# One row tile for both norm parts, weight loads ahead of the bias rows, a later strip load, and two early input chunks

## The reference, cut to what matters

```python
# first block, twice
h = rms_norm(x, norm_mix[l]); z = h @ w_in[l]
qa, ka, va, qi, ki, wi, cq, ckv, kr, ga, gb = split_cols(z)
qa, ka = rms_norm(qa), rms_norm(ka)              # per head of 64
y_a = sparse_indexed_attention(qa, ka, va, qi, ki, wi, rel_bias, 128)
cq, ckv = rms_norm(cq), rms_norm(ckv)            # latents of 384 and 256
qb, kb = up-projections, rope on 32 of 96, rms_norm per head of 96
y_b = latent_attention(qb, kb, vb)
x = x + (sigmoid(ga + ..) * (y_a @ w_proj_a) + sigmoid(gb + ..) * (y_b @ w_proj_b)) @ w_out[l]
h = rms_norm(x, norm_ffn[l]); u = causal_dwconv(h @ w_up[l], ..)
x = x + (silu(u[.., D_FF:]) * u[.., :D_FF]) @ w_down[l]
# second block, once: dilated attention, and attention over keys that are
# compressed (hid = gelu(blocks @ w1 + b1); keys = hid @ w2), selected, and in a window
# then gated feed-forward and a last rms_norm
```

## Time and profile before

| | us |
|---|---|
| median of three runs | 2419.99 |
| profiled execution | 2424.52 |
| its span, first to last instruction | 2422.7 |
| PE busy in the span | 2356.8 (97%) |
| POOL busy | 1592.8 (66%) |
| DVE busy | 1242.0 (51%) |
| ACT busy | 615.5 (25%) |
| mean granted TensorE clock | 0.996 |

### The profile page before, as it was taken

One profiled execution on the slowest core, in us unless ns is written; L12 is line 12 of the kernel. 1 busy time (PEld: TensorE's weight loads), 2 busy tenths in 40 slices (PEclk: granted clock), 3 DMA queues, 4 the chain that ended last, 5 costly groups with the idle time before them and its releaser, 6 DMA issues.

```text
span 2422.7 us, 34631 instructions
## 1 busy us (share of the span) xinstructions
PE 2356.8 (97%) x11150; PEld 1777.1 (73%) x11150; DVE 1242.0 (51%) x2116; ACT 615.5 (25%) x1349; POOL 1592.8 (66%) x818
## 2 busy tenths in 40 slices
PE   6999999999999999999999999999999999999997
PEld 4666578878888776665788788887777567887886
DVE  4576554366516536775543665165535755440442
ACT  4233620131101223336201311012321754000001
POOL 4563357777778775543577787777755427777774
PEclk9999999999999999999999999999999999999999
DMA  6222012223332322220122233323362003333232
GB/s 192 70 70 105 19 58 91 96 87 95 96 90 92 96 88 70 71 104 19 62 92 93 87 94 96 96 90 92 125 208 90 33 2 90 92 95 96 87 95 87
DMA packets 61586, 212.65 MB, mean 88 GB/s; under 512 B 6344, under 2 KB 6728, under 8 KB 61328
## 3 DMA queue, kind: packets, MB, share of 16 engines
q1 hardware_dynamic: 54368, 194.38, 25.8%
q10 hardware_dynamic: 7088, 16.58, 2.0%
HBM read 208.78 MB, written 10.01 MB: 90 GB/s over the span
## 4 chain that ended last, share of the span: by engine, by line
PE 88%; ACT 3%; DVE 2%; DMA 2%; issue 2%; DVEq 1%; POOL 1%; ACTq 0%; SPq 0%; POOLq 0%
PE out_tile L505 75%; PE turned L652 3%; PE stat L669 2%; DMA bias_rows<-bias_kept 1%; PE turned L629 1%; ACT sq L1138 1%; PE out_tile L824 1%; PE out_tile L829 1%; PE out_tile L1010 1%; PE out_tile L726 1%; ACT arena L1148 1%; PE out_tile L834 1%; DMA weight_ring<-stream 1%; DVEq L1449 0%; DMA x<-x_t 0%
## 5 line engine op out<-in xcount | busy, mean ns | idle before, releaser
L505 PE MATMUL out_tile<-arena_r,w_hi 128*128 128x512 f32 x5240 | 1656.8, 397 | 0.0
L505 PEld LDWEIGHTS out_tile<-arena_r,w_hi 128*128 128x128 f32 x5240 | 990.6, 189 | 239.8 <-issue 1.9
L505 PE MATMUL out_tile<-arena_r,w_lo 128*128 128x512 f32 x2620 | 1052.1, 402 | 21.0 <-POOL w_lo L1901 6.1
L1895 POOL TENSOR_TENSOR w_hi<-weight_ring,cst 128x1024 fp32r<-128x1024 f32 (+1 forms) x348 | 660.1, 1897 | 566.0 <-PE out_tile L505 486.6
L1901 POOL TENSOR_TENSOR w_lo<-weight_ring,w_hi 128x1024 fp32r<-128x1024 f32 (+1 forms) x348 | 853.0, 2451 | 26.7
L505 PEld LDWEIGHTS out_tile<-arena_r,w_lo 128*128 128x128 f32 x2620 | 495.2, 189 | 171.1 <-issue 29.2
L1427 DVE TENSOR_TENSOR x<-out_tile,x 128x512 f32<-128x512 f32 x72 | 49.8, 692 | 341.0 <-PE out_tile L505 340.9
L1249 ACT ACTIVATE work<-out_tile,p 128x512 f32<-128x512 f32 x88 | 66.0, 775 | 377.0 <-PE out_tile L505 264.4
L1363 DVE CAST arena_r<-work 128x512 f32 (+2 forms) x84 | 137.2, 1634 | 13.0 <-issue 11.8
L1365 DVE TENSOR_TENSOR arena_r<-work,arena_r 128x512 f32 (+2 forms) x84 | 136.4, 1624 | 13.4 <-issue 12.1
L1685 DVE SCALAR_TENSOR_TENSOR work<-out_tile,p,work 128x511 f32<-128x511 f32 x88 | 65.6, 746 | 137.6 <-ACT work L1249 137.6
(11 more groups left out here) (215 smaller groups left out, 1866.9 us busy)
## 6 DMA issues: line engine op xcount, KB each, us to landing
weight_ring<-stream SPq DMA_DIRECT2D x356, 512.0 KB, 3.5
arena<-bias_rows ACTq DMA_DIRECT2D x4, 2048.0 KB, 9.9
bias_rows<-bias_kept ACTq DMA_DIRECT2D x2, 2556.0 KB, 23.7
bias_rows<-bias_kept SPq DMA_DIRECT2D x1, 2556.0 KB, 14.7
x<-x_t SPq DMA_DIRECT2D x4, 512.0 KB, 9.1
arena<-w ACTq DMA_DIRECT2D x1, 2048.0 KB, 8.9
out_t<-arena SPq DMA_DIRECT2D x8, 256.0 KB, 2.2
cst<-consts SPq DMA_DIRECT2D x1, 576.0 KB, 14.1
```

What stands on the lines that cost most here:

```text
L505: ins = pe.matmul(out, l, r, start=start and n == 0, stop=stop and n == 2, **kw)
L1895: pool.tensor_tensor(blocks_of(w_hi[:, s % SPLIT, :], used), blocks_of(ring[:, s, :], used), cols(cst, C_ONE).unsqueeze(1).to_broadcast([P ...
```

## The change

The edits are four. (1) `rows_lo` is gone. The ones-columns of the constants are repeated 16 columns on, so that each group of 32 partitions holds its sums twice; a column C_LOWER of the constants is 0 in the first 16 rows of each group and -1 in the others; the last VectorE instruction of `row_inverse_root` turns the second copy into the lower part within the same tile `rows_both`; the 0/1 matrix has ones at both places, and `spread_rows` issues one matmul over 32 (or 64) rows in place of two over 4 (or 64). (2) SP issues the loads of ring round 1 ahead of its wait for the bias rows; its loop begins at round 2. (3) `load_strips(strips_b, 2, ...)` moves in ScalarE's stream from ahead of the tanh to behind the copies of the compressed keys and values and the load of the Exp table. (4) The upper and lower parts of chunks 0 and 1 of x are made right behind the square (and the adding) of chunk 3.

```diff
@@ -78,7 +78,8 @@
 C_BOTH = C_QUAD + 34
 C_VALID = C_BOTH + 34
 C_EPS = C_VALID + 1
-C_PERM = C_EPS + 1
+C_LOWER = C_EPS + 1
+C_PERM = C_LOWER + 1
 C_COS = C_PERM + P
 C_SIN = C_COS + S
 C_CMP = C_SIN + S
@@ -282,7 +283,6 @@
         p2 = sb("p2", [P, P2_N])
         sq = sb("sq", [P, 3, S])
         rstd = sb("rstd", [P, S])
-        rows_lo = sb("rows_lo", [P, S], F32R)
         spread_r = sb("spread_r", [P, 4 * P], F32R)
         newton = sb("newton", [P, S])
         work = sb("work", [P, 6, S])
@@ -316,7 +316,7 @@
         strips = chunks(24, 8)
         qi, ki = chunks(32, 4), chunks(36, 1)
         misc, kr_all = chunks(37, 1), chunks(38, 1)
-        rows_hi = arena_r[:, 39, :]
+        rows_both = arena_r[:, 39, :]
         cq, ckv = parts(40, 43), parts(46, 48)
         maskb = arena[:, 43, :]
         sel = chunks(50, 3)
@@ -476,12 +476,16 @@
             for s in range(1, RING):
                 sp.dma_start(ring[:, s, :], stream[s]).then_inc(landed[s], 16)
             sp.dma_start(cst[:, C_COS:C_N], consts[:, C_COS:C_N]).then_inc(load_cst, 16)
+            for s in range(RING):
+
+                sp.wait_ge(weights_split, s + 1)
+                sp.dma_start(ring[:, s, :], stream[RING + s]).then_inc(landed[s], 16)
             sp.wait_ge(rows_ready, len(bias_parts))
             sp.dma_start(rows[0:HEADS, :], biasrow[0:HEADS, 0:WIN]).then_inc(rows_kept, 16)
             sp.dma_start(rows[HEADS:3 * HEADS, :], biasrow[:, WIN:2 * WIN]).then_inc(rows_kept, 16)
             sp.wait_ge(rows_kept, 32)
             repeat_rows(sp, 0)
-            with sp.Fori(1, total // RING) as i:
+            with sp.Fori(2, total // RING) as i:
                 for s in range(RING):
 
                     sp.wait_ge(weights_split, i * RING + (s - RING + 1))
@@ -623,11 +627,10 @@
                         pe.wait_ge(latent_ready, L * 2 + min(n, 2))
                     out = turn[n % 2]
                     kind, c = key if norm != "lat" else (key, ("cq", "ckv").index(key))
-                    for rows, start in ((rows_hi, True), (rows_lo, False)):
-                        g = slice(64 * c, 64 * c + 64) if kind in ("qr", "kr") else slice(32 * c, 32 * c + 4)
-                        at = dict(ka=P, kn=P, qr=2 * P, kr=3 * P).get(kind, 0)
-                        ins = pe.matmul(out[:, :], spread_r[g, at:at + P], rows[g, :], start=start, stop=not start)
-                    ins.then_inc(spread_done, 1)
+                    g = slice(64 * c, 64 * c + 64) if kind in ("qr", "kr") else slice(32 * c, 32 * c + 32)
+                    at = dict(ka=P, kn=P, qr=2 * P, kr=3 * P).get(kind, 0)
+                    pe.matmul(out[:, :], spread_r[g, at:at + P], rows_both[g, :], start=True, stop=True)\
+                      .then_inc(spread_done, 1)
 
                 def row_sums():
                     return latent_sums, head_sums, rope_sums, spread_rows
@@ -1149,12 +1152,18 @@
                            .then_inc(sec.turn_taken, 1)
 
             act.wait_ge(load_p1, 16)
+            def first_upper(k):
+                raw_upper(0, k, lambda k: cols(p1, PC_MIX + k), h_mix)
+
             for k in range(DC):
                 if k % (DC // XPARTS) == 0:
                     act.wait_ge(load_x[k // (DC // XPARTS)], 16)
                 square(0, MIX, k)
-            for k in range(DC):
-                raw_upper(0, k, lambda k: cols(p1, PC_MIX + k), h_mix)
+                if k == 3:
+                    first_upper(0)
+                    first_upper(1)
+            for k in range(2, DC):
+                first_upper(k)
             act.wait_ge(load_first, 16)
 
             with act.Fori(0, LAYERS) as L:
@@ -1305,13 +1314,13 @@
             for name, half in enumerate((slice(0, HD), slice(HD, P))):
                 ins = act.activation(work[half, 0, 0:P], stat[0][half, name * P:(name + 1) * P], ACT.Copy)
             ins.then_inc(hidden_copied, 1)
-            load_strips(strips_b, 2, strips_branch_in)
             act.wait_ge(gelu_arg, 1)
             act.activation(work[:, 3, 0:P], work[:, 2, 0:P], ACT.Tanh, scale=GELU_C).then_inc(gelu_tanh, 1)
             act.wait_ge(compressed_done, 1)
             act.activation(k_cmp[:, 0, 0:64], turn[1][:, 0:64], ACT.Copy)
             act.activation(v_cmp[:, 0, 0:P], turn[1][:, 64:64 + P], ACT.Copy).then_inc(compressed_copied, 1)
             load_table(ACT.Exp)
+            load_strips(strips_b, 2, strips_branch_in)
             for b in range(QB):
                 act.wait_ge(cmp_masked, b + 1)
                 act.activation(work[:, b, 0:2 * P], work[:, b, 0:2 * P], ACT.Exp, scale=-1.0).then_inc(cmp_exp, 1)
@@ -1380,7 +1389,7 @@
 
             def row_inverse_root(L, norm, rows=P):
 
-                t, upper, lower = stat[ROW_STAT[norm]][0:rows, :], rows_hi[0:rows, :], rows_lo[0:rows, :]
+                t, both = stat[ROW_STAT[norm]][0:rows, :], rows_both[0:rows, :]
                 dve.wait_ge(row_root, L * len(ROW_NORMS) + ROW_NORMS.index(norm) + 1)
                 plain(dve)
                 dve.scalar_tensor_tensor(out=t, in0=t, scalar=EPS, in1=newton[0:rows, :], op0=ALU.add, op1=ALU.mult)
@@ -1389,9 +1398,10 @@
                 dve.drain()
                 dve.tensor_tensor(t, t, rstd[0:rows, :], ALU.mult)
                 dve.drain()
-                dve.tensor_copy(upper, t)
+                dve.tensor_copy(both, t)
                 dve.drain()
-                dve.tensor_tensor(lower, t, upper.bitcast(F32), ALU.subtract).then_inc(row_ready, 1)
+                dve.scalar_tensor_tensor(out=both, in0=both.bitcast(F32), scalar=cst[0:rows, C_LOWER:C_LOWER + 1], in1=t,
+                                         op0=ALU.mult, op1=ALU.add).then_inc(row_ready, 1)
 
             def spread_wait(L, key):
                 n = SPREAD_AT[key]
@@ -1499,7 +1509,10 @@
 
             for k in range(DC):
                 add_square(0, MIX, k, newton[:, :])
-            for k in range(DC):
+                if k == 3:
+                    raw_lower(0, 0, h_mix)
+                    raw_lower(0, 1, h_mix)
+            for k in range(2, DC):
                 raw_lower(0, k, h_mix)
             dve.wait_ge(rows_done, len(bias_parts))
             for bank, to, rows_n, table, at, width in bias_parts:
@@ -2017,10 +2030,12 @@
     c[:, C_ID:C_ID + P] = np.eye(P)
     c[:, C_ONE:C_ONE + P] = 1
     for half in range(2):
-        c[64 * half:64 * half + 64, C_PAIR + 2 + half] = 1
-        for quarter in range(2):
-            c[64 * half + 32 * quarter:64 * half + 32 * quarter + 32, C_QUAD + 2 + quarter] = 1
-        c[:, C_BOTH + 2 + half] = 1
+        for at in (2, 18):
+            c[64 * half:64 * half + 64, C_PAIR + at + half] = 1
+            for quarter in range(2):
+                c[64 * half + 32 * quarter:64 * half + 32 * quarter + 32, C_QUAD + at + quarter] = 1
+            c[:, C_BOTH + at + half] = 1
+    c[:, C_LOWER] = -(np.arange(P) % 32 // 16)
     inv = np.float32(10000.0) ** (-np.arange(16, dtype=np.float32) / 16)
     ang = np.arange(S, dtype=np.float32)[None, :] * inv[:, None].astype(np.float32)
     for i in range(0, P, 32):
@@ -2051,7 +2066,7 @@
 def _spreads():
 
     t = np.zeros((P, 4 * P), np.float32)
-    for g in range(0, P, 32):
+    for g in range(0, P, 16):
         for e in range(2):
             t[g + e, 64 * e:64 * e + 64] = 1
             t[g + 2 + e, P + 64 * e:P + 64 * e + 64] = 1
```

## The result

The changed kernel takes 2391.10 us, median of 4 runs (2390.75 to 2393.93), beside 2420.05 for the kernel before (2419.77 to 2420.97, now 4 runs). The ratio is 0.9875, 95% interval 0.9863 to 0.9886: faster by 28.9 us where 26.7 were forecast. Applied to 2419.99 the ratio gives 2389.7, just under the low end of the forecast's range. The profiled execution took 2393.93 us, its span is 2392.1; against 2424.52 and 2422.7 that is 30.6 less. More came than the sum held, and not all from where it said: in the profiled execution one of its terms came to a fifth (0.5 of 2.4 us), and something that it put at nothing, the place of a tile, is worth some 8 us.

A forecast was written before the change was run, and what follows sets the result against it. PE's stream was taken as the bound, busy 2356.8 of 2422.7 us. The terms 9.7 + 2.4 + 6.8 + 7.8 = 26.7 us, taken from the median 2419.99, gave 2393.3 us, range 2390.0 to 2401.0.

The forecast's parts named there:

- rival D: Operands start elsewhere in SBUF after the constants edit, slowing the L505 products; 3.3 ns each eats the gain; chance 0.03.
- Edit 4, forecast 2.4: At the start: chunks 0 and 1 made earlier let PE's first product and the root come sooner; 2.4 us, bounds 1 and 2.5.
- Edit 2, forecast 6.8: Early weight loads: PE's wait for POOL's tile 4 and the slow stretch behind it go; 6.8 us, bounds 5.0 and 7.2.
- rival C: Bias repeat takes 10 us longer, tile 8 lands late, PE stands 3.5 us: 2399 us; chance 0.05.
- Edit 1, forecast 9.7: Spreads: 44 lower matmuls leave PE's stream, 10.3 us, less 0.6 at the attention's entry; 9.7 us.
- The loss at the attention's entry: VectorE takes the first scores late, so PE loses 0.3 us in each layer, bounds 0 and 0.7; 0.6 in all.
- Rival A: Spreads not on the path: PE only reaches VectorE earlier at each attention; 2403.0, or 2398 for half; chance 0.12.
- Edit 3, forecast 7.8: Compressor: the tanh no longer waits behind the strips, so PE's wait and slow products go; 7.8 us, bounds 3.5 and 8.
- the two POOL instructions that it named: Compressor's gelu: POOL's split instructions from 1791.18 to 1793.08 and until 1795.56 hold VectorE's chain until 1795.6 at the latest.
- rival B: Gelu chain caught again by POOL's instruction at 1796.81, PE stands 1.6 us, up to 3 more: 2395 to 2398; chance 0.12.

The follow-up runs named there:

- e1: The kernel before with an unused tile of 32 bytes put ahead of the arena and nothing else; 2418.11 us against 2426.73, ratio 0.9966.
- e2: The changed kernel with an unused tile of 32 bytes ahead of the arena; 2393.34 us, ratio 0.9860 to the kernel before.
- e15: The changed kernel with the second ring round again behind the bias rows, tiles left in place; 2399.83 us, ratio 0.9903 to the kernel before.
- e7: The changed kernel with rows_lo back and two matmuls a spread, the arena's distance kept modulo 256; 2399.36 us, ratio 0.9880 to the kernel before.
- e16: The changed kernel with ScalarE loading the strips ahead of the tanh again; 2395.71 us, ratio 0.9887 to the kernel before.
- e6: The changed kernel with 64 unused bytes ahead of the arena; 2350.32 us, ratio 0.9682 to the kernel before.
- e11: The changed kernel with w_hi moved by 32 bytes and the arena at 99968 as in e6; 2391.93 us, ratio 0.9862 to the kernel before.

## Why the prediction was right or wrong

- **The step that failed** is the weighing of rival D: "No row shows a dependence of a product's rate on where its operand stands", and so 0.2334 us for each product before and after, in every term and in the sum. The edit of the constants did move the arena, as the rival said, but I let it go one way only, to slower, and gave it 0.03. It came with the other sign: each of the 1245 products took 0.95 ns less, and e1 shows that the place does it and is worth 8.0 us, which the sum put at nothing. Without them the kernel would have taken about 2398, inside the range.
- **Edit 4, forecast 2.4.** ScalarE, VectorE and PE's first product moved nearly as forecast (first product 17.46 for 17.1, the root's table load 24.05 for 23.7). In the profile only 0.5 us of it arrived, because VectorE's cast met a POOL instruction; e2, whose cast did not, has its inverse root 2.7 sooner. The sum left out that these casts can be caught, though it had weighed the same thing for edit 3. Whether they are is chance: they were in 2 of 4 profiles without edit 4 as well.
- **Edit 2, forecast 6.8.** Right: 6.7 in the profile, and 6.6 by e15. SP's queue did as told, and POOL began on tile 8 at 67.53 without a wait for a load, so rival C did not come. The clock behind the hole, 0.53 before, is 1.00 from 44 to 60 us.
- **Edit 1, forecast 9.7.** Right in mechanism: 9.2 by the traces of e7. The loss at the attention's entry is 10.3 - 9.2 = 1.1 and not 0.6. In the profiled execution only 7.7 of the 9.2 arrived, since its first pass has a slow stretch of 1.5 us that the profile of before has not; whether the edit brings it about stays open. Rival A did not come.
- **Edit 3, forecast 7.8.** Right: 8.0 in the profile, 7.4 by e16, with the two POOL instructions that it named and the chain's last step 1.0 us ahead of PE; rival B did not come. The sum took 0.95 us off the nine small products and 2.1 off the 24 behind them for the lower clock, 0.52 from 1802.30 to 1809.00; with the hole gone the clock is 1.00 from 1777 to 1784 us, and they took 1.18 and 2.04 less. How the two POOL instructions bear on the chain was the author's estimate from the earlier trace rows; the profile after shows the two long VectorE instructions end at 1772.66 and 1775.04, POOL's at 1772.50 and 1774.99.

That the forecast came as near as 3.9 us to the profile is partly luck, for its errors cancel in part: 8.0 more for the place, 1.9 less for edit 4, 2.0 less for edit 1 in this execution, 0.5 less for the other two (6.7 for 6.8 and, by e16, 7.4 for 7.8). That makes 3.6 of the 3.9.

## What to carry to other kernels

When an edit changes the size of any tile, write down where the two operands of the main product stand before and after, and try pads of 32 to 224 bytes between them: here one of 64 bytes was worth 42 us, more than the four edits together. Ask of each short VectorE instruction on the path what POOL may be running beside it (here a cast of 0.23 us took 1.87). And read a term of one or two microseconds from several executions, since a cast or a clock can fall either way.

## What the runs showed of the hardware

- Of the six distances tried (modulo 256), a 128x512 fp32r product with 128x128 weights was quickest where moving operand and weights lay a multiple of 256 bytes apart in a partition: 1245 of them took 284.9 to 285.4 us (seven kernels), at the other five 289.6 to 292.0 (13 kernels), up to 2.5% more.
- With both tiles moved from e6's places by 32 or 128 bytes, the distance kept, 1245 products took 285.28 and 285.18 us for 284.96; with the weights alone moved by 32 they took 290.77 (e11).
- In the changed kernel a stretch at half clock (granted 0.50 between 124 and 126 us) began while PE was busy, behind 16 products over 32 rows and 32 columns of weights; in e16, behind the same products, the clock stayed at 1.00 (5.93 and 4.39 us for 18 products).
- A cast of VectorE took 1.87 us where it began 0.11 behind the start of a POOL instruction, and 0.23 in the kernel before, where POOL was idle when it began.
